# Experts in stretches of 64 sorted places, high and low part in one stationary

## The reference

```python
def hier_moe(h, wg, bg, we, be, w_gate, w_up, w_down):
    """Top-1 expert group, then top-2 experts within it; gate = p(group) * softmax(top-2 logits)."""
    ...
    gates = jax.nn.softmax(top_v, axis=-1) * pg
    ids = (g_sel * EXPERTS_PER_GROUP + top_i).reshape(-1).astype(jnp.int32)
    order = jnp.argsort(ids)
    tok = order // TOP_K
    xs = xf[tok]
    sizes = jnp.bincount(ids, length=N_EXPERTS).astype(jnp.int32)
    hg = lax.ragged_dot(xs, w_gate.astype(xs.dtype), sizes)
    hu = lax.ragged_dot(xs, w_up.astype(xs.dtype), sizes)
    ys = lax.ragged_dot(jax.nn.silu(hg) * hu, w_down.astype(xs.dtype), sizes)
    ys = ys * gates.reshape(-1)[order][:, None].astype(ys.dtype)
    y = jax.ops.segment_sum(ys, tok, num_segments=t)
```

## Time and profile before

| | |
|---|---|
| median of 3 runs | 1080.19 us |
| the profiled execution | 1080.93 us |
| its span, first to last instruction | 1079.1 us |
| TensorE busy | 1034.6 us (96%) |
| VectorE busy | 842.9 us (78%) |
| ScalarE busy | 665.2 us (62%) |
| GpSimd busy | 33.0 us (3%) |
| DMA | 253.61 MB |

### The profile page before, as it was taken

How to read it: one execution, slowest core, us unless ns; L and a number is a source line. 1 busy time by engine, 2 the same in 40 slices (tenths; PEclk the granted TensorE clock), 3 DMA queues, 4 the chain that set the end, 5 groups by cost and what they waited for, 6 DMA issues and landing times. The chain is left out here.

```text
span 1079.1 us, 14950 instructions
## 1 busy us (share of the span) xinstructions
PE 1034.6 (96%) x5574; PEld 872.7 (81%) x5574; DVE 842.9 (78%) x1091; ACT 665.2 (62%) x832; POOL 33.0 (3%) x40
## 2 busy tenths in 40 slices
PE   7999999999998899989889999999999999999996
PEld 6777999999998777889778787878787777878775
DVE  5855766766777556677757889999999899999977
ACT  5554655555555645556333677777777777777764
POOL 1001000000000100100020000000000000000000
PEclk9999999999999999999999999999999999999999
DMA  9634545646424443233311789989998998999881
GB/s 349 244 117 137 194 169 184 196 157 234 156 91 150 158 144 130 81 118 118 117 32 34 285 327 368 371 348 390 349 388 351 374 363 352 378 359 386 339 318 43
DMA packets 82711, 253.61 MB, mean 235 GB/s; under 512 B 4160, under 2 KB 42176, under 8 KB 62656
## 3 DMA queue, kind: packets, MB, share of 16 engines
q1 hardware_dynamic: 82624, 252.50, 62.2%
HBM read 251.44 MB, written 1.05 MB: 234 GB/s over the span
## 5 line engine op out<-in xcount | busy, mean ns | idle before, releaser
L1021 DVE TENSOR_TENSOR WL<-raw,WH 128x2048 fp32r<-128x2048 f32 x232 | 497.5, 2175 | 110.0 <-ACT WH L543 109.7
L543 ACT ACTIVATE WH<-raw 128x2048 fp32r<-128x2048 f32 x232 | 421.5, 1823 | 91.2 <-PE bank L1910 74.9
L1908 PE MATMUL bank<-WH,MXH 128*128 128x512 f32 x552 | 219.4, 397 | 1.6 <-DVE CV L1316 0.9
L1910 PE MATMUL bank<-WH,MXL 128*128 128x512 f32 x552 | 216.0, 391 | 0.0
L1909 PE MATMUL bank<-WL,MXH 128*128 128x512 f32 x552 | 215.5, 390 | 0.0
L1908 PE MATMUL bank<-HTH,WH 128*128 128x256 f32 x576 | 166.1, 288 | 6.2 <-DVE CV L1316 2.6
L1910 PE MATMUL bank<-HTH,WL 128*128 128x256 f32 x576 | 163.6, 284 | 0.0
L1909 PE MATMUL bank<-HTL,WH 128*128 128x256 f32 x576 | 163.6, 284 | 0.0
L1908 PE MATMUL bank<-WH,HTH 128*128 128x512 f32 x348 | 139.7, 401 | 7.2 <-DVE HTL L1044 2.4
L1909 PE MATMUL bank<-WL,HTH 128*128 128x512 f32 x348 | 137.1, 394 | 0.0
L1908 PEld LDWEIGHTS bank<-WH,MXH 128*128 128x128 f32 x552 | 104.4, 189 | 23.2 <-issue 2.3
(11 more groups left out here) (393 smaller groups left out, 1098.6 us busy)
## 6 DMA issues: line engine op xcount, KB each, us to landing
raw<-in_exp_w_up SPq DMA_DIRECT2D x52, 1024.0 KB, 7.6
raw<-in_exp_w_gate SPq DMA_DIRECT2D x52, 1024.0 KB, 8.1
raw<-in_exp_w_down SPq DMA_DIRECT2D x52, 1024.0 KB, 6.7
raw<-in_w_in SPq DMA_DIRECT2D x34, 1024.0 KB, 5.1
raw<-in_w_up SPq DMA_DIRECT2D x22, 1024.0 KB, 5.4
raw<-in_w_down SPq DMA_DIRECT2D x11, 1024.0 KB, 5.2
raw<-in_w_out SPq DMA_DIRECT2D x8, 1024.0 KB, 5.0
raw<-in_w_o SPq DMA_DIRECT2D x4, 1024.0 KB, 5.6
```

Source lines behind the costliest of these rows:

```text
L543: e.activation(WH[i % HL][:, 0:n], raw[i % RAW][:, 0:n], ACT.Copy).then_inc(a_wh, 1)
L1021: e.tensor_tensor(l, r, h.bitcast(F32), ALU.subtract).then_inc(v_wl, 1)
L1908: e.matmul(out_, ah, bh, start=start, stop=False)
L1910: return e.matmul(out_, al, bh, start=False, stop=stop)
```

## The change

- A unit is an expert and a stretch of 64 of its sorted places, beginning at its first place or a multiple of 64 behind it. The places are not shifted; an expert with more than 64 has several units.
- The 64 places' high parts and the same 64 places' low parts make one stationary of 128 columns. It is multiplied with WH and with WL (`two`): rows 0 to 63 of the result come from the high part, rows 64 to 127 from the low part, and low times low is in it too.
- `turn_hidden` adds the two halves of rows while it turns: eight full float32 products of 64 columns with a constant matrix `same`, in place of four transposes. Gate and norm are applied to the rows ahead of it on ScalarE (`gate_rows`, `up_rows`), SiLU and the product come after it.
- Each unit's outputs are split and selected to tokens in the next but one unit (`back`, eight products) into four PSUM banks that hold all of them to the end. The tiles' sums and the 48 products at the end fall away.
- GpSimd copies the low features (`features_low`) and makes the turned selection of each unit (`selection`), and in the beginning the diagonals for the rows of positions, gates and norms, which TensorE spreads over partitions (`route_rows`).
- The table of units comes from comparing each count with 0, 64, 128 and so on.
- At the end the last norm goes by quarters, and both engines write halves of the output.

```diff
-NT = 5
-NS = 128 * NT
-UNITS = 36
+W = 64
+NS = 512
...
-LEAST = 4
+LEAST = 8
...
+            def features_low(u):
+
+                at = e.value_load(TBI[u:u + 1, 1:2], min_val=0, max_val=NS - 1)
+                e.wait_ge(*((p_used, unit_base(u - 2) + 4) if u > 1 else (v_xst, 8)))
+                e.tensor_copy(XC[u % 2][:, :, 1, :], XSP[:, :, 1, bass.ds(at, W)]).then_inc(g_xc, 1)
+
+            def selection(u):
+
+                if u > 1:
+                    e.wait_ge(p_back, u - 1)
+                if u:
+                    e.wait_ge(g_sel, 2 * u)
+                e.tensor_scalar(S1, PR, SLOT[:, u:u + 1], None, ALU.is_equal).then_inc(g_sel, 1)
+                e.wait_ge(g_sel, 2 * u + 1)
+                e.tensor_tensor(SELT[u % 2], S1[:, 0, :], S1[:, 1, :], ALU.add).then_inc(g_sel, 1)
...
+            def two(out_, x, wh, wl, start, stop):
+
+                e.matmul(out_, x, wh, start=start, stop=False)
+                return e.matmul(out_, x, wl, start=False, stop=stop)
...
+            def turn_hidden(u, w=TBK):
+
+                e.wait_ge(a_gu, 2 * u + 2)
+                if u and w == TBK:
+                    e.wait_ge(v_yl, 2 * u)
+                for b, v in enumerate((GS, US_)):
+                    for k in range(4):
+                        at = b * 256 + k * W
+                        m = e.matmul(bank[w][:, at:at + W], v[:, k:512:4], same, start=True, stop=True)
                 m.then_inc(p_hidT, 1)
...
             def unit(u):
                 i = unit_base(u)
                 if u > 1:
+                    features(u)
                     split(i)
                     split(i + 1)
-                turn_hidden(u - 1)
+                    for c in range(2):
+                        outputs_high(u - 2, c)
                 split(i + 2)
                 split(i + 3)
...
+                gate_rows(u)
+                silu(u - 1)
                 split(i + 4)
+                hidden_high(u - 1)
                 split(i + 5)
+                up_rows(u)
...
             def unit(u):
                 i = unit_base(u)
                 if u > 1:
...
                     split(i)
                     split(i + 1)
-                turn_hidden(u - 1)
-                if u > 1:
-                    e.wait_ge(p_used, unit_base(u - 1) + 6)
-                    gather_y(u - 2)
+                    for c in range(2):
+                        outputs_low(u - 2, c)
+                gates(u)
                 split(i + 2)
                 split(i + 3)
+                gate_hidden(u - 1)
                 split(i + 4)
+                hidden_low(u - 1)
                 split(i + 5)
-                gate_hidden(u)
...
+            def unit(u):
+                i = unit_base(u)
+                e.wait_ge(a_xch, u + 2)
+                e.wait_ge(g_xc, u)
+                e.wait_ge(a_gu, 2 * u - 1)
+                product(u, GB, i)
+                turn_hidden(u - 1)
+                if u > 1:
+                    back(u - 2)
+                product(u, UB_, i + 2)
+                down(u - 1, i + 4, range(4))
```

More of the change, by code:

```diff
@@ L119 @@
 SQ = numbered([("mix", t) for t in range(T)] + [("ffn", i) for i in range(3)] + [("n1", i) for i in range(6)]
[L120 to L123, removed]
+              + [("n2", c, t) for c in range(2) for t in range(T)] + [("out", c, t) for c in range(2) for t in range(T)])
+V_ROUTE = numbered(["ge2", "mm", "dm", "first", "pos", "gates", "units", "lists", "slots"])
+A_ROUTE = numbered(["ge2", "dm", "pos", "rows"])
+P_ROUTE = numbered(["counts", "lists", "pos", "rows"])
 HROW = numbered(["ffn", "n1"])
@@ L373, in build @@
[L373 to L394, removed]
@@ new lines, in vector @@
+            for k in range(8):
+                e.wait_ge(a_xst, k + 1)
+                e.scalar_tensor_tensor(out=XSP[:, k, 1, 0:NS], in0=bank[GATB[k]][:, :], scalar=ptcol("norm2_by_row", k),
+                                       in1=XSP[:, k, 0, 0:NS].bitcast(F32), op0=ALU.mult,
+                                       op1=ALU.subtract).then_inc(v_xst, 1)
+            split(NP + 2)
+            e.wait_ge(p_route, P_ROUTE["lists"])
+            e.tensor_scalar(MINE, bank[6][:, NU:2 * NU], const("place", 1), None, ALU.is_gt).then_inc(own.up(), 1)
@@ new lines, in gpsimd, with more @@
+            features_low(1)
+            e.wait_ge(v_route, V_ROUTE["slots"])
+            e.wait_ge(a_route, A_ROUTE["pos"])
+            selection(0)
+            def unit(u):
+                if u > 1:
+                    features_low(u)
+                selection(u)
+            def more(u):
+                with e.If(count > u):
+                    unit(u)
+                    if u + 1 < UNITS:
+                        more(u + 1)
+            for u in range(1, LEAST):
+                unit(u)
@@ L1904, in gpsimd @@
+            more(LEAST)
             row_powers("out")
@@ L2410, in down @@
+            def down(u, i, ks, banks=YB):
+                if ks[0] == 0:
+                    e.wait_ge(v_hil, u + 1)
+                for k in ks:
+                    native = k == 3 and banks == YB
                     if k % 2 == 0:
                         wh, wl = piece(i + k // 2, 2)
[L2412 to L2417 removed]
@@ L2463, in tensor @@
-            unit(0)
-            turn_selection()
+                    for c in range(2):
+                        hs = slice(c * 512, (c + 1) * 512)
+                        if native:
+                            w = raw[(i + 1) % RAW][:, PC // 2:PC]
+                            m = e.matmul(bank[banks[c]][:, :], both(HID[u % 2][:, k]).bitcast(F32), w[:, hs], start=False,
+                                         stop=True)
+                        else:
+                            m = two(bank[banks[c]][:, :], both(HID[u % 2][:, k]), wh[:, k % 2, hs], wl[:, k % 2, hs], k == 0,
+                                    k == 3)
```

699 lines of the change are left out of this document (295 added, 404 removed).

## The result

The changed kernel takes 1210.46 us (median of 4 runs, 1204.65 to 1210.98) against 1080.32 for the kernel before on the same chip: ratio 1.118, interval 1.113 to 1.123. The forecast was 1110, with a range to 1150: the sign was right, the size far off. The profiled execution has a span of 1208.9 us where the forecast's sum had 1109.1, 99.8 more.

A forecast was written before the change was run, and what follows sets the result against it. TensorE bounds the kernel before; after, a loop through TensorE, ScalarE and VectorE plus some GpSimd gives the period. 642.4 + 25 x 17.2 + 36.7 = 1109.1 us span, forecast 1110, range 1098 to 1150.

The forecast's parts named there:

- Number of units: Expert stage: 28 units in place of 26, two experts having more than 64 tokens; a rival with 26 had 0.04.
- The loop: Each unit: first gate product through up product, ScalarE's up rows, features and split, then VectorE's low half; 16.96 us.
- a share for GpSimd: Period of a unit: GpSimd's work partly added to VectorE's, so 17.2 us, between 16.96 and 17.5.
- The gap: TensorE, once a unit ahead of the first gate product: a wait of 1 to 2 us, ended by that piece's low half.
- a gap there: TensorE's gap ahead of the down product instead: would mean the hidden's chain or VectorE binds, and the period forecast is wrong.
- the eight turns at 0.23 us: TensorE, each unit: eight full-precision products with 64 columns, 1.86 us in place of 0.39 for four turns.
- The head and the end: Before unit 2's first gate product: 642.4 us; from the last unit's first gate product to the finish: 36.7 us.
- VectorE and GpSimd: Each unit: VectorE 14.8 us, lengthened by GpSimd's operations that exclude its own; in a row 16.45, 17.5 or 20.4 us.
- Low halves over 2.29 where GpSimd is busy: Sign on VectorE: low halves take longer than their usual 2.29 us while GpSimd works beside them.
- middle price of 2.7: GpSimd's copy, comparison and addition per unit: 2.7 us together, between 1.65 and 5.6.
- TensorE's own pace (15.4): Rival: TensorE's work sets the period in the expert stage, 15.4 us, time 1065 us; chance 0.05.
- GpSimd as the bound: Rival: dear copy and comparison, VectorE plus GpSimd 20.4 us a unit, 1190 us; chance 0.15 including all from 18.3.

The follow-up runs named there:

- both edits: Changed kernel with turns reading neighbouring columns and ScalarE's split of the next gate piece ahead of the up rows' evacuation: 1112.04 us, ratio 1.028.
- the selection cut: Against the kernel whose turns read neighbouring columns: GpSimd compares and adds 8 places in place of 256 from the third unit on; 1121.55 us, one run.
- contiguous turns: Changed kernel with ScalarE writing gate and up rows in the order the turns read, 128 neighbouring columns each: 1127.79 us, ratio 1.042.
- contiguous ones of the same length: Against the kernel whose turns read neighbouring columns: the same eight products issued twice over; 1170.61 us, one run.
- filling the gap: Changed kernel with one added full-precision product of 512 columns on constants ahead of each unit's gate product: 1213.15 us, ratio 1.120.
- the gap moved: Changed kernel with ScalarE's split of the next unit's first gate piece ahead of the up rows' evacuation: 1168.26 us, ratio 1.080.

## Why the prediction was wrong

- **Number of units: right.** 28, and the two more cost 33.4 us of periods with both edits.
- **The loop: right**, in place and order, and nearly in size. With the turns near their forecast cost (1.70 for 1.86) the period is 17.24 where 17.2 was forecast. That it agrees to 0.04 is partly luck: the loop alone was put at 16.96, the rest was a share for GpSimd, and with the selection cut, which left the period at 17.23, no such share shows. Against 16.96 the selection was 0.14 longer, the gate product 0.08, and up rows to the gate product 0.2, the turns 0.16 shorter. The gap stands where it was said to; with contiguous turns a second one, 0.58, stands ahead of the down product. The forecast had named a gap there as a sign that something else sets the period; but cutting the selection changed that gap and left the period.
- **The step that failed is the eight turns at 0.23 us.** The row it was taken from the earlier trace rows had a contiguous stationary; here it is every fourth column. A record takes 0.22 us and not 0.11, a weight load 329 ns and not 192. That is 1.67 us a unit, some 42 in 25 periods. The number of columns was not at fault: 64 take 0.11 a record when contiguous, as 33 did. The warning was in the trace of before, in a view that the prediction did not use. The transposes of the hidden read every fourth column too, and the data are what a transpose loads as weights (one that turns 8 columns loads 8). Their weight loads take 208 ns, those of a transpose of neighbouring columns (L2395) 140; at 0.10 apart the products hardly showed it:

```profile
L2404 PEld LDWEIGHTS bank<-cn,CV x104: 196/208/219, 622.0 to 1053.3; 128*128 128x128 f32 x104
...
L2395 PEld LDWEIGHTS bank<-cn,HTH x10: 138/140/142, 620.8 to 621.9; 128*128 128x128 f32 x10
...
L2194 PEld LDWEIGHTS bank<-cn,BIG x2: 85/86/87, 367.4 to 367.6; 128*8 128x8 f32 x2
```

- **What the sum had no term for: the clock.** In the trace of before the stage stood at 1.00, and the forecast kept it. The selection takes 3.39 us at 0.50 and 1.95 at 1.00. The changed kernel's own first two periods, where the clock did not fall, are 19.0 us (17.2 and the turns), the later ones 20.5: the clock costs 1.5 us a unit, some 34 in 23 periods. The runs show that it goes with the strided turns (contiguous ones of the same length leave it at 1.00, filling the gap does not help). They do not show why: after the same strided turns it did not fall in the first two periods, nor in about half of the units when the gap moved.
- **The head and the end: 9.9 us too short each.** Unit 2's first gate product came at 652.30, not 642.4. Single executions differ here: in the five kernels that have both edits, and nearly the same head, it came between 644.1 and 650.0, so a part of the 9.9 may be this execution's. In it the native gate product began 3.0 late, behind a load, and ran 9.8 us, not 7.0, more than half of it at 0.50 after TensorE had stood 5.4 us:

```profile
607.70 9.81 PE L2425 MATMUL bank<-raw,MXH 128*128 128x512 f32 x16 [5.41 <-ACT MXH L905]
608.00:610.00 2.00, 2.00 (x3) 0.84 (x3) 2.00 (x4) 1.10 (x3) 0.25 (x1) 0.50 0.02 8
```

  Before, TensorE was never idle there. Unit 1 then took 21.6 where some 17.6 were forecast. The end, from 1162.28, took 46.6, not 36.7: from the last product to the end 9.5 us and not 6.2, the last turns 4.6 and not 1.9, with a wait ahead of their second half, and down products at the low clock:

```profile
1181.32 1.85 PE L2383 MATMUL bank<-cn,CV 128*128 128x64 f32 x8
1184.08 1.85 PE L2383 MATMUL bank<-cn,CV 128*128 128x64 f32 x8 [0.91 <-issue]
1187.95 0.80 PE L2346 MATMUL bank<-WH,HTL 128*128 128x512 f32 x1 [2.02 <-DVE HTL L1700]
```

  With contiguous turns both are still 7.7 too short (650.05, and 44.4 to the end).
- **VectorE and GpSimd: the mechanism right, the payer wrong.** The Trainium skill's rule ("SBUF — State Buffer", "Who interferes with whom") says that a VectorE instruction with two SBUF inputs and a GpSimd instruction that reads SBUF contend. The traces agree where GpSimd comes second: 3.48 us for a comparison whose shortest record is 1.57. They agree where a GpSimd copy or addition comes first (0.96 for 0.42), but not for a low half that begins behind a running comparison and keeps its 2.29. "Low halves over 2.29 where GpSimd is busy" did not come: in the changed kernel GpSimd pays. By its shortest records GpSimd alone needs 1.57 + 0.74 + 0.60 = 2.9 us, near the middle price of 2.7. VectorE's share, about 1 us in the contiguous kernel, lies in its slack, and only with both edits do 0.34 reach the period.
- **Rivals.** TensorE's own pace (15.4) came in no run; the shortest period, 16.10, with half of the gate loads and most of GpSimd's work left out, is still a loop's. 28 x 16.10 = 451 us is more than 26 x 17.19 = 447; at the estimated 15.7 the 28 units would be 440, so that way of winning was narrow but is not disproved. GpSimd as the bound did not happen, though the time came out beyond it.

The sum: 9.9 + 25 x 3.2 + 9.9 = 99.8. No run of all the computation beats the kernel before.

## What to carry to other kernels

A price taken from a row holds for that row's access pattern: before using it, compare the step of both operands. The clock of the kernel before need not be that of the kernel after, even where TensorE's records show no gap: give it a rival with a price, here 1.5 us a unit on top of the 1.7 of the turns that it came with. And compare the count of units times the period before looking at anything else: at the shortest period that any of these runs showed, 28 units are no shorter than 26 were at the old one. A TensorE that is recorded as busy without a gap may still wait: compare the distances between starts.

## What was not expected of the hardware

- A full-precision product with a stationary of every fourth column takes 0.22 us a record in place of 0.11, its weight load 329 ns in place of 192, at a granted clock of 1.00.
- The weight loads of the float32 transposes of before take 208 ns with every fourth column and 140 with neighbouring ones, while the transposes stand 0.10 apart all the same.
- The clock fell from 2.4 to 1.2 GHz at the end of 3.5 us in which TensorE was recorded as busy without a pause; in two units of the same trace it did not.
- A GpSimd operation beside a VectorE low half is recorded as busy while it stands: 3.48 for 1.57 (comparison), 2.41 for 0.61 (copy). A low half that begins 0.9 us behind a running comparison is not held up: 2.29, as alone.
